# A two-layer transformer trunk on one core: later first weight units in the head, shift and scale of two chunks summed past the first FFN norm, other ada buffers, first silu in other memory

## The reference

```python
c_act = silu(c)
for i in range(2):
    mod = c_act @ ada_w[i] + ada_b[i]                  # 6 vectors of 2048
    sh_a, sc_a, g_a, sh_f, sc_f, g_f = split(mod, 6)
    h = x * (1 + sc_a) + sh_a
    y = mla(h) if i == 0 else fox(h)
    x = layer_norm(alpha * x + (1 + g_a) * y, ln1_g, ln1_b)
    h = x * (1 + sc_f) + sh_f
    y = (silu(h @ w1) * (h @ w3)) @ w2
    x = layer_norm(alpha * x + (1 + g_f) * y, ln2_g, ln2_b)
# mla: lat = h @ w_down; q from 512, k and v from 512 normed columns of lat, 16 heads; out @ w_o
```

## Time and profile before

| what | value |
|---|---|
| median of 3 runs | 2253.83 us (2253.12 to 2254.78) |
| the profiled execution: its own time | 2257.64 us |
| its span in the trace | 2255.8 us |
| TensorE busy | 2170.6 us, 96% |
| VectorE busy | 1568.3 us, 70% |
| ScalarE busy | 999.5 us, 44% |
| GpSimd busy | 104.6 us, 5% |
| mean granted TensorE clock | 0.991 |

### The profile page before, as it was taken

One profiled execution on the slowest core, in us unless ns is written; L12 is line 12 of the kernel. 1 busy time (PEld: TensorE's weight loads), 2 busy tenths in 40 slices (PEclk: granted clock), 3 DMA queues, 4 the chain that ended last, 5 costly groups with the idle time before them and its releaser, 6 DMA issues.

```text
span 2255.8 us, 24976 instructions
## 1 busy us (share of the span) xinstructions
PE 2170.6 (96%) x9778; PEld 1771.2 (79%) x9778; DVE 1568.3 (70%) x1776; ACT 999.5 (44%) x1321; POOL 104.6 (5%) x207
## 2 busy tenths in 40 slices
PE   6789899999999999999999999999999999999997
PEld 2368777888888888888788888878888888888886
DVE  5789889877677877778876555678775555454556
ACT  1066545444443344443544555554444433444433
POOL 2111100000000000000000000000000000000000
PEclk9899999999999999999999999999999999999999
DMA  9998996788988888889667667747876656656563
GB/s 385 418 374 326 337 395 234 277 290 302 265 325 323 319 322 299 298 301 343 227 237 266 225 224 226 283 167 271 288 285 164 231 194 195 193 188 189 178 236 119
DMA packets 145879, 604.43 MB, mean 268 GB/s; under 512 B 23905, under 2 KB 24161, under 8 KB 119393
## 3 DMA queue, kind: packets, MB, share of 16 engines
q1 hardware_dynamic: 109282, 397.27, 50.3%
q0 software_dynamic: 27648, 201.34, 24.3%
q10 hardware_dynamic: 8832, 4.23, 0.7%
HBM read 600.64 MB, written 2.13 MB: 267 GB/s over the span
## 4 chain that ended last, share of the span: by engine, by line
PE 84%; DVE 8%; DMA 5%; ACT 1%; issue 1%; SPq 0%; DVEq 0%; ACTq 0%
PE ps L1477 52%; PE ps L1483 26%; DMA ada_head<-in_ada_w 3%; DVE wlo L910 2%; PE ps L1494 2%; DVE ada_w L935 2%; DMA ada_w<-in_ada_w 1%; PE ps L1464 1%; PE ps L1666 1%; DMA raw<-in_mla_w_o 1%; DMA raw<-in_mla_w_uk 1%; DVE ada_low L935 1%; DVE ada_head L935 1%; PE ps L1642 0%; PE ps L1691 0%
## 5 line engine op out<-in xcount | busy, mean ns | idle before, releaser
L910 DVE TENSOR_TENSOR wlo<-raw,whi 128x1024 fp32r<-128x1024 f32 (+1 forms) x717 | 869.6, 1218 | 601.0 <-ACT whi L542 600.2
L542 ACT ACTIVATE whi<-raw 128x1024 fp32r<-128x1024 f32 (+1 forms) x717 | 755.8, 1056 | 1081.3 <-PE ps L1483 1019.8
L1477 PE MATMUL ps<-whi,hT_hi 128*128 128x512 f32 x1880 | 587.6, 394 | 2.3 <-DVE hT_lo L1247 2.3
L1477 PE MATMUL ps<-whi,hT_lo 128*128 128x512 f32 x1880 | 579.8, 390 | 0.0
L1483 PE MATMUL ps<-wlo,hT_hi 128*128 128x512 f32 x1880 | 502.9, 389 | 0.0
L1477 PEld LDWEIGHTS ps<-whi,hT_lo 128*128 128x128 f32 x1880 | 352.9, 188 | 74.4
L1483 PEld LDWEIGHTS ps<-wlo,hT_hi 128*128 128x128 f32 x1880 | 352.9, 188 | 73.9
L1477 PEld LDWEIGHTS ps<-whi,hT_hi 128*128 128x128 f32 x1880 | 348.7, 188 | 72.2 <-DVE hT_lo L1247 2.7
L935 DVE CUSTOM_DVE_ANT_0 ada_w<-ada_w,c_bc,cols 128x2048 f32<-128x2048 f32 x144 | 337.6, 2345 | 24.8 <-DMA ada_w<-in_ada_w 14.6
L1477 PE MATMUL ps<-whi,uT_hi 128*128 128x512 f32 x656 | 202.3, 390 | 0.0
L1477 PE MATMUL ps<-whi,uT_lo 128*128 128x512 f32 x656 | 201.9, 389 | 0.0
(11 more groups left out here) (244 smaller groups left out, 1504.7 us busy)
## 6 DMA issues: line engine op xcount, KB each, us to landing
raw<-in_ffn_w SPq DMA_DIRECT2D x528, 512.0 KB, 4.4
ada_w<-in_ada_w POOLq DMA_DIRECT2D x144, 1024.0 KB, 6.0
raw<-in_fox_w_in SPq DMA_DIRECT2D x96, 512.0 KB, 4.3
ada_head<-in_ada_w POOLq DMA_DIRECT2D x17, 1024.0 KB, 20.3
raw<-in_mla_w_o SPq DMA_DIRECT2D x32, 512.0 KB, 8.8
raw<-in_fox_w_o SPq DMA_DIRECT2D x32, 512.0 KB, 4.4
gate<-in_ada_w POOLq DMA_DIRECT2D x13, 1024.0 KB, 10.9
ada_low<-in_ada_w POOLq DMA_DIRECT2D x10, 1024.0 KB, 10.4
```

Of the source, the lines that this page charges most:

```text
L542: nc.scalar.activation(split_hi(pl.unit)[:, 0:n], raw[:, s, 0:n], ACT.Copy).then_inc(hi_ready, 1)
L910: nc.vector.tensor_tensor(split_lo(pl.unit)[:, 0:n], raw[:, s, 0:n], split_hi(pl.unit)[:, 0:n].bitcast(F32), ALU.subtract).then_inc(lo_rea ...
L1477: nc.tensor.matmul(ps[:, 2 * pair + t, 0:width], a[:, t * P:(t + 1) * P], w_hi, start=(first and c == 0 and a is hi), stop=False)
```

## The change

- **Head.** SP holds back the first weight units until ada chunk 30 is in. Chunk 31 comes in two halves with a sum each. ACT and DVE copy `lat` after 2 and 1 split units instead of 5; the other splits stand between the turns; the second `turn_latent` stands behind unit 0; the ada behind the copies stands behind `lat_rstd`.
- **Attention 0.** Ticks 2, 6, 10 and 14 have one `ada()` instead of two; these 4 are done in layer 1's attention. The buffer tables change (five buffers until chunk 57, not 53; then the order 0, 1, 2). G_A is turned by TensorE into 16 rows in tick 9, copied, and stored as rows of 512 bytes.
- **First FFN norm.** The columns 14 and 15 of shift and scale (4 ada chunks) are summed behind the norm, and the turn of these two chunks waits for them (`late_cols`). TensorE does 4 units of w1, 4 of w3, and then w1 and w3 alternately. `scale_xa` is split, its second part later. The first silu goes to `sums`, and waits only for its product.

```diff
@@ tables
+             + [(0, G_A, c) for c in range(KC)]
+             + [(0, q, c) for c in range(KC) for q in (SC_F, SH_F)]
...
-ADA_WIDE_UNTIL = 54
+LATE_C = KC - UC
+ADA_EARLY = ADA_HEAD + KC + 2 * LATE_C
+ADA_WIDE_UNTIL = 58
...
-            slots.append((2, 0, 1)[(n - ADA_WIDE_UNTIL) % 3])
+            slots.append((0, 1, 2)[(n - ADA_WIDE_UNTIL) % 3])
...
+def one_ada(i):
+
+    return i % 4 == 2 and i < H
@@ SP
+            sp.wait_ge(ada_in[ADA_SLOT[ADA_HEAD - 2]], 16 * ada_loads(ADA_HEAD - 2))
@@ ACT, norm_turn
+                    if k > 0 or m < SPLIT - 1:
+                        turn_affine(8 + UC * m)
+                if k == 0:
+                    units(2 * SPLIT)
+                    act.wait_ge(late_cols, 1)
+                    turn_affine(LATE_C)
@@ ACT, attention
+                    if rotary and i == GATE_TICK:
+                        act.wait_ge(gate_turned, 1)
+                        nc.scalar.activation(gate_turn[:, :], ps[0:KC, 7, S:S + P], ACT.Copy
+                                             ).then_inc(gate_turn_ready, 1)
+                        act.wait_ge(gate_turn_ready, 1)
+                        act.dma_start(rows[pl.gate].rearrange("(c p) -> c p", p=P), gate_turn[:, :]
+                                      ).then_inc(gate_row, 16)
@@ ACT, ffn
-                        if (n, i) == (0, 0):
+                        silu = silu_of(n, i)
+                        if (n, i) == (0, 1):
                             act.wait_ge(xa_updated, 2 * l + 1)
@@ ACT, head
+            split()
+            split()
+            lat_copy(0)
+            for b in range(2):
+                turn_gain(qlT_hi, b, 0)
+            lat_copy(1)
+            lat_squares(0)
+            split()
+            for b in range(2):
+                turn_gain(kvT_hi, b, LC)
+            split()
+            lat_squares(1).then_inc(ssq_ready, 1)
+            ahead()
@@ DVE, norm_turn
+                if k == 0:
+                    for m in range(SPLIT - 1):
+                        units(1)
+                        turn_affine(8 + UC * m)
+                    units(2)
+                    ada()
+                    for _ in range(2 * UC - 1):
+                        units(1)
+                        ada()
+                    affine_cols(*columns, LATE_C, KC).then_inc(late_cols, 1)
+                    units(4)
+                    turn_affine(LATE_C)
+                    for t in range(T):
+                        units(1)
+                        scale_g(t, k)
+                    units(1)
+                    return
@@ DVE, attention
-                    if layer == 0:
+                    if layer == 0 and not one_ada(i) or layer == 1 and one_ada(i) and pl.ada < ada_end(1, SH_F):
                         ada()
@@ PE, norm_turn
+                pair_free(pl.block + 1)
+                for m in range(SPLIT):
+                    unit((pl.block + 1) % 2, NB, both(m), m == 0, False)
                 for m in range(SPLIT, PAIRS):
                     pe.wait_ge(turned_out, first + m + 1)
-                    product(m, KC, hT_hi, hT_lo)
+                    unit(pl.block % 2, NB, both(m), False, m == PAIRS - 1)
+                    unit((pl.block + 1) % 2, NB, both(m), False, m == PAIRS - 1)
+                pl.block += 2
@@ PE, ahead of the first projections
-            turn_latent(1)
             for k in range(MLA_GROUP):
+                if k == 1:
+                    turn_latent(1)
```

More of the change, by code:

```diff
@@ L100, in ada_loads @@
 def ada_loads(n):
-    return sum(s == ADA_SLOT[n] for s in ADA_SLOT[:n + 1])
+    return sum(s == ADA_SLOT[n] for m, s in enumerate(ADA_SLOT[:n + 1]) if m != ADA_HEAD - 1)
 def ada_slot_free(n):
@@ L266, in trunk @@
     pinv = new("pinv", [P, 2, 2])
+    gate_turn = new("gate_turn", [KC, P])
     assert at[0] <= nc.sbuf_usable_end, (at[0], nc.sbuf_usable_end)
@@ L342, in trunk @@
         gate_row = sem("gate_row")
+        gate_turned = sem("gate_turned")
+        gate_turn_ready = sem("gate_turn_ready")
+        late_cols = sem("late_cols")
         gate_copied = sem("gate_copied")
@@ L436, in load_ffn @@
                     for i in range(first, first + nb):
+                        if (l, i) == (0, 0):
+                            for name in ("ffn_w1", "ffn_w3"):
+                                for j in range(SPLIT):
+                                    load(A[name][l, j])
+                            for j in range(SPLIT, PAIRS):
+                                for name in ("ffn_w1", "ffn_w3"):
+                                    load(A[name][l, j])
+                            continue
                         for name in ("ffn_w1", "ffn_w3"):
@@ L767, in attention @@
                     if i == H // 2:
-                        gate_out(layer, G_A)
+                        if layer == 1:
+                            gate_out(layer, G_A)
                     if i == H:
@@ L828, in _, with lat_copy, lat_squares @@
                                      ).then_inc(h_ready, 1)
-            ahead()
-            for which, dst in enumerate((qlT_hi, kvT_hi)):
+            def lat_copy(which):
                 act.wait_ge(lat_ready, which + 1)
                 nc.scalar.activation(lat[:, which, 0, :], ps[:, 2 * which, :], ACT.Copy).then_inc(lat_act, 1)
-                for b in range(2):
-                    turn_gain(dst, b, which * LC)
-            act.wait_ge(lat_dve, 2)
-            for which in range(2):
+            def lat_squares(which):
+                act.wait_ge(lat_dve, which + 1)
                 for t in range(T):
@@ L1111, in norm_turn @@
             def norm_turn(k, columns):
-                affine_cols(*columns)
+                if k == 0:
+                    chain(affine_cols(*columns, 0, LATE_C))
+                else:
+                    chain(affine_cols(*columns))
                 first_half(k)
@@ L1289, in w_o @@
                     units(1)
-                    if layer == 0 and k == 0:
+                    if layer == 0 and k == 0 and pl.ada < ADA_EARLY:
                         ada()
             def ffn(l):
-                units(PAIRS - SPLIT - T)
+                if l > 0:
+                    units(PAIRS - SPLIT - T)
                 for n, nb in enumerate(FF_PASSES):
@@ L1297, in ffn @@
                     for i in range(nb):
-                        if (n, i) != (0, 0):
+                        if (l, n, i) == (0, 0, 1):
+                            own()
+                            for t in range(T):
+                                units(2)
+                                scale_b(t)
+                            units_with_ada(PAIRS - 2 * T)
+                        elif (n, i) != (0, 0):
                             units_with_ada(PAIRS)
@@ L1355, in _, with lat_copy @@
             ada(ADA_HEAD - 4)
-            ahead()
-            for which, (hi, lo) in enumerate(((qlT_hi, qlT_lo), (kvT_hi, kvT_lo))):
+            def lat_copy(which):
                 dve.wait_ge(lat_ready, which + 1)
                 nc.vector.tensor_copy(lat[:, which, 1, :], ps[:, 2 * which + 1, :]).then_inc(lat_dve, 1)
-                for b in range(2):
-                    turn_gain(hi, lo, b, which * LC)
-            ada()
+            split()
+            lat_copy(0)
+            for b in range(2):
+                turn_gain(qlT_hi, qlT_lo, b, 0)
+            lat_copy(1)
+            split()
+            split()
+            for b in range(2):
+                turn_gain(kvT_hi, kvT_lo, b, LC)
+            ahead()
             dve.wait_ge(ssq_ready, 1)
@@ L1378, in _ @@
             w_o(0)
[L1379 removed]
+            ada(max(0, ADA_EARLY - pl.ada))
             norm_turn(0, (0, 0, 0, SH_F, SC_F))
@@ L1644, in attention @@
                     gap(gaps[0])
+                    if rotary and i == GATE_TICK:
+                        pe.wait_ge(ada_done, ada_end(0, G_A))
+                        pe.wait_ge(o_lo, i - 3)
+                        nc.tensor.transpose(ps[0:KC, 7, S:S + P], mod[:, G_A, :], ident[:, :]
+                                            ).then_inc(gate_turned, 1)
                     if rotary and i < H and i % 2 == 0:
@@ L1690, in attention @@
                             pe.wait_ge(qp_copied, i // 2 + 1)
+                        if rotary and i == GATE_TICK:
+                            pe.wait_ge(gate_turn_ready, 1)
                         nc.tensor.matmul(ps[:, 7, 0:S], v_tile(0, i - 3), pT[:, m % 2, 0:S],
@@ L1730, in ffn @@
                                 turn(lambda t, c: u[:, t, c * P:(c + 1) * P], UC * b)
-                        for j in range(PAIRS):
-                            product(j, KC, hT_hi, hT_lo)
+                        if (l, n, i) != (0, 0, 0):
+                            for j in range(PAIRS):
+                                product(j, KC, hT_hi, hT_lo)
                     for b in range(4):
```

93 lines of the change are left out of this document (66 added, 27 removed).

## The result

The changed kernel takes 2243.88 us (median of 5 runs, 2243.36 to 2244.27), the kernel before beside it 2254.78 us (5 runs, 2253.12 to 2258.17). The ratio on record is 0.9946, 95% interval 0.9935 to 0.9958: faster by 0.4 to 0.65%, clear of the noise though small. (The quotient of these two medians is 0.9952; over all 50 timed executions of the kernel before, those of the experiments included, its median is 2256.46 us, and 2243.88 is 0.9944 of that.) The span went from 2255.8 to 2242.2 us, 13.6 less. I had predicted 2238.4 us, inside a range of 2230 to 2246, and 15.4 us less on the trace.

A forecast was written before the change was run, and what follows sets the result against it. VectorE was taken to set the pace in the head and attention 0. Head -1.9, attention 0 -14.9, norm +0.9 and +0.5 sum to -15.4 us; off the 2253.8 us median that gives 2238.4, range 2230 to 2246.

The forecast's parts named there:

- the forecast itself: Whole kernel: the predicted case, 2234 to 2242 us, chance 0.58.
- the loads stay the limit: Rival, attention 0: VectorE's DMA waits come back by half in ticks 12 and 13; 2244 to 2245 us, chance 0.17.
- head, at VectorE's ada of 137.58: Head: VectorE reaches this ada at 135.7, 1.9 us earlier; bounds 0 and -5.5.
- ticks 1 to 4: Attention 0: the second ada of tick 2 falls away, 2.3 us off TensorE's wait at 186.7.
- ticks 6 and 8: Attention 0: tick 6's wait of 0.6 us stays, tick 8's of 0.9 goes; -0.9 us.
- tick 10, clock, ticks 11 and 12: Attention 0: waits from VectorE's DMA waits go, -4.6 in tick 10 and -4.6 in 11 and 12; half clock goes, -2.5.
- (a): First FFN norm: split, table load and silu outlast the last w3 unit, +0.9 us; +2.3 with the skill page's drain.
- (b): First FFN norm: two more 1 MB loads start during `w_o` and may delay a unit; +0.5 us, bounds 0 and 2.6.
- (c): First FFN norm: the late turn of chunks 14 and 15 finishes 2 us ahead of need and costs 0.
- term (1): Head: weight loads held back and chunk 31's sum halved start the last h32 at 114.5, not 117.2; 2.7 us.
- Term (2): Head: fewer splits ahead of the `lat` copy and the new order bring `lat_rstd` at 131.1, 4.2 us earlier.
- The signs: Profile: `lat_rstd` about 4 us earlier, unit 0 about 7, tick 12's turn near 248, store of G_A within some 3 us.

The follow-up runs named there:

- u_hold: The changed kernel without SP's wait ahead of the first weight units; 2246.74 us, ratio 0.9956 to the kernel before.
- b_store: The kernel before with only the new store of G_A added; 2251.18 us, ratio 0.9973.
- u_both: The changed kernel with the old buffer tables and the old element-wise store of G_A together; 2254.91 us, ratio 0.9993.
- x_best: The changed kernel with a spare one-column silu ahead of ScalarE's last split, the old store of G_A and no SP wait; 2245.39 us, ratio 0.9947.
- b_table: The kernel before with only the new buffer tables, the slow store kept; 2245.69 us, ratio 0.9957.

## Why the prediction was right, and where its sizes were off

The direction was right, and so was attention 0 as the stage that would give most; the largest term, ticks 10 to 12, came close. But 2243.88 us lies outside the 2234 to 2242 that I gave to the forecast itself, next to the 2244 to 2245 of *the loads stay the limit*, and that rival did not happen: VectorE waits for no ada load in ticks 12 and 13. What is missing lies in the head, in ticks 10 to 12, and in the base from which I subtracted.

| step | predicted, us | trace after - before | what the runs say |
| --- | --- | --- | --- |
| head, at VectorE's ada of 137.58 | -1.9 | +0.1 | -0.5 for the whole head: hold -1.2, order +0.8 |
| ticks 1 to 4 | -2.3 | -1.9 | right |
| ticks 6 and 8 | -0.9 | -1.6 | wrong reason: the wait stays; clock |
| tick 10, clock, ticks 11 and 12 | -11.7 | -10.1 | tables or store |
| first silu (a) | +0.9 | +0.9 | right |
| weight loads in w_o (b) | +0.5 | -1.4 | wrong sign |
| late turn (c) | 0 | 0 | right |
| sum | -15.4 | -14.0 | 13.6 at the end; 0.4 is spread over the rest |

**The head is the step that was mis-sized**, and in it term (1), the 2.7 us by which the last h32 was to come earlier. It measured 0.0 between the two traces and 1.2 over all of them. The bound that I missed is chunk 30: the hold starts only when it is in (SP issues its first unit at 111.47, VectorE starts the sum of chunk 30 at 111.48), and behind it VectorE has that sum and both halves to do, 2.3 + 2.6 us, which ends at 116.5. The halves take 2.57 us for 2.35, so they alone win nothing: u_hold has them and starts the h32 with the kernels of before. Term (2) was right: 2.7 us taken off its start, my 131.1 for `lat_rstd` becomes 133.8, and it came at 133.02. And the -1.9 without those 2.7 is +0.8, for the ada that now stands behind `lat_rstd` with nothing beside it: just what the new order costs at tick 2 (u_hold against the kernels with the old head). With the hold's measured 1.2 the prediction's own sum gives -0.4, and the runs say -0.4 to -0.5. So the new order was priced right; it is a loss, which the size of (1) hid.

**Attention 0.** The -2.3 of tick 2's ada came, as 1.9. The 0.9 of tick 8 did not: VectorE idles 1.9 us ahead of 205.93, where tick 6 has lost its ada, for ScalarE's copy of a unit; the slack was there, and the wait stayed, so it is one of the chain between the engines and not of VectorE's load. What moved ticks 6 and 8 was the clock in tick 4, 1.6 us. That I had a saving there was luck: the kernels with the old tick 2 run without this episode in two of five traces, so only a part of the 1.6 is the change's own, and I had it in no term. In ticks 10 to 12 the waits left are 0 and 0.5 us, and the clock is 1.00 where it was 0.61 and 0.53, as predicted; the turn of G_A costs 0.7 us of wait and 0.3 of work, what I had called under 1 us. I had written that the wait "is gone with the slow store and with five buffers until chunk 57", and gave the 83 GB/s to the store. That was right, but I had it as one cause with a help; the runs show two that must meet in the changed kernel, and that the tables alone give most of it in the one before. The first of VectorE's three waits was never the store's: it stays, 3.2 us, in b_store.

**The norm.** (a) came out at 0.89 us. That rests on the row that showed no drain: after, the table load of 405.63 ends at 406.91 and the silu starts at 406.92. The Trainium skill, "ScalarE: Activation LUTs", section What ACT_TABLE_LOAD costs, adds about 1.4 us of drain, by which my estimate of (a) would have been 2.3. The measurement decides: neither the row ahead of the load (it ends at 405.61) nor the one behind leaves room for a drain. (b) had the wrong sign: the last units of w_o waited 1.4 us for their `wlo` before, and 0 after. It is no gain of the change either: the wait is 0.4 us in u_both, 0.6 in u_hold, 0.8 in x_best and none in b_table and the nine others, so it comes and goes from trace to trace. (c) The late turn is done at 399.8, with 10 units from 374.2 on needed at 401.4: 1.6 us of margin, for 2 expected.

**The base.** 15.4 for 13.6 is only 1.8 us of the 5.5 between 2238.4 and 2243.88. The other 3.7 come from taking a saving worked out on one execution off a median that was 3.8 us lower. Most of that was the median and not the execution: it came from three runs, and over all 50 timed executions of the kernel before the median is 2256.46 us, 2.6 above it and only 1.2 below the 2257.64 of the profiled one. That one had its clock episode of tick 4 and its `wlo` wait, 3.0 us together, which other kernels with the same code there run without; how often the kernel before has them is not shown, as no other execution of it was traced.

**The signs.** As said: no TensorE wait over 2 us between ticks 6 and 16, full clock in 225 to 255, and a wait of 0.9 us ahead of the second FFN block. Off in size: `lat_rstd` 2.1 us earlier for 4, unit 0 5.6 for 7, tick 12's turn at 251.15 for 248, and the new store of G_A landing in 5.7 us for 3.

## What to carry to other kernels

Where one engine issues loads in order into a rotating set of buffers, write down for every load how many loads older the one is whose buffer it takes: a step from five to two held the ada loads for 16 us just ahead of a slow store, and two lines in a table were worth 10 to 12 us. The changed kernel holds its ada loads as long, 17 us, later, and pays nothing, so ask what follows such a stand, and how much work the filled buffers still hold. A store that slows the loads for 8 us costs nothing while the buffers hold more than 8 us of work. Such a pair of causes is tested with each undone and with both undone, as here the single edits said "nothing" or little for either. And base a forecast on what several executions have in common: stalls behind clock episodes and late loads of one trace are not all there to be won, and a median of three runs was 2.6 us off.
